# Attention gates of a hybrid layer: exp(-ln(1 + exp(-z))) per group of columns instead of one sigmoid per key head

## What is computed

```python
aq, ak, av, rq, rf_fwd, rf_bwd, ri, rg, za, zr = jnp.split(h @ w_in, IN_SPLITS, axis=-1)
...
attn = block_attention(q, k_all, v_all)
...
merged = jax.nn.sigmoid(za) * attn + jax.nn.sigmoid(zr) * rec
return merged @ w_o, k, v, S_f, S_b
```

## Time and profile before

| | |
|---|---|
| time, median of 3 runs | 2664.16 us (2663.98 to 2665.03) |
| the profiled execution, its own time | 2663.92 us |
| its span, first to last instruction | 2662.1 us |
| PE busy | 2557.1 us, 96% |
| DVE busy | 1697.6 us, 64% |
| ACT busy | 1031.3 us, 39% |
| POOL busy | 837.3 us, 31% |
| granted clock of PE over the span | 0.988 |

### The profile page before, as it was taken

How to read it: one execution, slowest core, us unless ns; L and a number is a source line. 1 busy time by engine, 2 the same in 40 slices (tenths; PEclk the granted TensorE clock), 3 DMA queues, 4 the chain that set the end, 5 groups by cost and what they waited for, 6 DMA issues and landing times. The chain is left out here.

```text
span 2662.1 us, 40132 instructions
## 1 busy us (share of the span) xinstructions
PE 2557.1 (96%) x14417; PEld 2358.6 (89%) x14417; DVE 1697.6 (64%) x2807; ACT 1031.3 (39%) x1924; POOL 837.3 (31%) x779
## 2 busy tenths in 40 slices
PE   5999999999998999999999999999999999999997
PEld 2799999999997977788778776798999999999997
DVE  4147456646748368787687677446776677766775
ACT  4233323323323257666666667423112222222214
POOL 1123132223223433433433325633322322322322
PEclk8999999999999999999999999999999999999999
DMA  8611111111111200010010012302111111111111
GB/s 319 201 33 44 36 50 42 44 33 50 36 38 31 57 19 9 25 39 9 25 47 9 1 53 62 113 31 64 40 47 39 39 47 39 39 47 39 39 32 72
DMA packets 164538, 135.94 MB, mean 51 GB/s; under 512 B 18492, under 2 KB 142300, under 8 KB 164444
## 3 DMA queue, kind: packets, MB, share of 16 engines
q1 hardware_dynamic: 163228, 129.99, 15.7%
q10 hardware_dynamic: 1216, 4.72, 0.5%
HBM read 120.41 MB, written 14.29 MB: 51 GB/s over the span
## 5 line engine op out<-in xcount | busy, mean ns | idle before, releaser
L388 PE MATMUL mix_ps<-act_hi,w_hi 128*128 128x384 f32 (+1 forms) x1320 | 444.1, 336 | 6.1 <-ACT conv L2492 3.0
L389 PE MATMUL mix_ps<-act_lo,w_hi 128*128 128x384 f32 (+1 forms) x1320 | 442.9, 336 | 0.0
L390 PE MATMUL mix_ps<-act_hi,w_lo 128*128 128x384 f32 (+1 forms) x1320 | 442.7, 335 | 0.0
L388 PE MATMUL proj_ps<-act_hi,w_hi 128*128 128x384 f32 x1152 | 406.4, 353 | 1.1 <-ACTq L741 1.1
L390 PE MATMUL proj_ps<-act_hi,w_lo 128*128 128x384 f32 x1152 | 386.5, 336 | 0.0
L389 PE MATMUL proj_ps<-act_lo,w_hi 128*128 128x384 f32 x1152 | 386.4, 335 | 0.0
L2602 DVE SCALAR_TENSOR_TENSOR resid_t<-mix_ps,mod,resid_t 128x384 f32<-128x384 f32 (+2 forms) x640 | 273.9, 508 | 134.5 <-PE mix_ps L390 134.5
L1944 DVE TENSOR_TENSOR probs_lo<-mix_ps,probs_hi 128x512 fp32r<-128x512 f32 x324 | 222.7, 688 | 142.4 <-ACT mix_ps L1739 138.8
L1738 ACT ACTIVATE probs_hi<-mix_ps 128x512 fp32r<-128x512 f32 x324 | 193.6, 598 | 183.9 <-PE mix_ps L1538 182.1
L388 PEld LDWEIGHTS mix_ps<-act_hi,w_hi 128*128 128x128 f32 x1320 | 248.8, 189 | 11.7 <-issue 5.4
L564 POOL CAST w_hi<-w_raw 128x1024 fp32r<-128x1024 f32 x48 | 79.2, 1649 | 571.2 <-PE proj_ps L390 531.3
(11 more groups left out here) (301 smaller groups left out, 5409.0 us busy)
## 6 DMA issues: line engine op xcount, KB each, us to landing
w_raw<-in_w_in SPq DMA_DIRECT2D x64, 512.0 KB, 3.8
w_raw<-in_w_up SPq DMA_DIRECT2D x44, 512.0 KB, 3.8
ada_w<-in_ada_w SPq DMA_DIRECT2D x7, 2048.0 KB, 15.8
w_raw<-in_w_down SPq DMA_DIRECT2D x22, 512.0 KB, 3.6
q_k_dec<-in_ada_w SPq DMA_DIRECT2D x5, 2048.0 KB, 8.1
out<-xy SPq DMA_DIRECT2D x9, 512.0 KB, 2.7
w_raw<-in_w_o SPq DMA_DIRECT2D x8, 512.0 KB, 5.3
xy<-in_x_sample SPq DMA_DIRECT2D x8, 512.0 KB, 6.9
```

The source lines that it names most:

```text
L388: nc.tensor.matmul(out, w_hi, x_hi, start=(k == 0), stop=False)
L389: nc.tensor.matmul(out, w_hi, x_lo, start=False, stop=False)
L390: return nc.tensor.matmul(out, w_lo, x_hi, start=False, stop=last)
```

## The change

`gate_out` and `first_gate_out` no longer copy a group out of PSUM. They write exp(-z) there, then ln(1 + x) in place, then exp(-x) in place, which together are 1 / (1 + exp(-z)). A group is so three ACT instructions of 128 by 384 instead of one, each waiting for the one before. `gate_sigmoid` and the table loads around it are gone, four sigmoids of 128 by 2304 and eight loads in all; exp and ln stay in one table. The semaphore `za_sig` now counts groups.

```diff
+                def gate_rest(kv, n, z):
+                    nc.scalar.activation(z, z, ACT.Ln, bias=1.0).then_inc(za_ln, 1)
+                    act.wait_ge(za_ln, 6 * kv + n + 1)
+                    nc.scalar.activation(z, z, ACT.Exp, scale=-1.0).then_inc(za_sig, 1)
+
                 def first_gate_out(n):
                     act.wait_ge(proj_done, NT + n + 1)
                     u, g = divmod(n, NG)
-                    nc.scalar.activation(ZA[:, u, g * G:(g + 1) * G], ps[:, B_PROJ + (NT + n) % 2, 0:G], ACT.Copy).then_inc(proj_out, 1)
+                    z = ZA[:, u, g * G:(g + 1) * G]
+                    nc.scalar.activation(z, ps[:, B_PROJ + (NT + n) % 2, 0:G], ACT.Exp, scale=-1.0).then_inc(proj_out, 1)
+                    act.wait_ge(proj_out, NT + n + 1)
+                    gate_rest(0, n, z)
 
                 def gate_out(kv, n):
                     act.wait_ge(f_done, F_AT["g", kv, n] + 1)
                     act.wait_ge(mix_ok, 2 * kv)
                     u, g = divmod(n, NG)
-                    nc.scalar.activation(ZA[:, u, g * G:(g + 1) * G], ps[:, B_F, 0:G], ACT.Copy).then_inc(f_out, 1)
+                    z = ZA[:, u, g * G:(g + 1) * G]
+                    nc.scalar.activation(z, ps[:, B_F, 0:G], ACT.Exp, scale=-1.0).then_inc(f_out, 1)
+                    act.wait_ge(f_out, F_AT["g", kv, n] + 1)
+                    gate_rest(kv, n, z)
...
-                def gate_sigmoid(kv):
-                    act.wait_ge(f_out if kv else proj_out, F_AT["g", kv, 5] + 1 if kv else NT + 6)
-                    nc.scalar.activation(ZA[:, :, :], ZA[:, :, :], ACT.Sigmoid).then_inc(za_sig, 1)
...
                     if kv:
                         inverse_ln(s - 1)
                         inverse_exp(s - 1)
-                        gate_sigmoid(kv - 1)
-                        nc.scalar.preload_act_table_set(LN_EXP)
...
-                    if s == NSTEP - 5:
-                        gate_sigmoid(NKV - 1)
-                        nc.scalar.preload_act_table_set(LN_EXP)
```

More of the change, by code:

```diff
@@ L1048, in phase2 @@
         r_ln, r_est, r_chk, r_ref, att_ok = sem("a_r_ln"), sem("a_r_est"), sem("a_r_chk"), sem("a_r_ref"), sem("a_att_ok")
-        za_sig, za_mul, rec_in, mix_ok, mix_store = sem("a_za_sig"), sem("a_za_mul"), sem("a_rec_in"), sem("a_mix_ok"), sem("a_mix_store")
+        za_ln, za_sig, za_mul, rec_in, mix_ok, mix_store = sem("a_za_ln"), sem("a_za_sig"), sem("a_za_mul"), sem("a_rec_in"), sem("a_mix_ok"), sem("a_mix_store")
         mixed_in, mh_ok, ml_ok, last_rec = sem("a_mixed_in"), sem("a_mixed_hi"), sem("a_mixed_lo"), sem("a_last_rec")
@@ L1350, in last_mix @@
                     if c == 0:
-                        pool.wait_ge(za_sig, NKV)
+                        pool.wait_ge(za_sig, 6 * NKV)
                         pool.wait_ge(last_rec, 32)
@@ L1963, in gate @@
                     dve.wait_ge(att_ok, NS * (kv + 1))
-                    dve.wait_ge(za_sig, kv + 1)
+                    dve.wait_ge(za_sig, 6 * (kv + 1))
                     for j in range(2):
@@ L2074, in last_mix @@
                     if c == 2:
-                        dve.wait_ge(za_sig, NKV)
+                        dve.wait_ge(za_sig, 6 * NKV)
                         dve.wait_ge(last_rec, 32)
```

## The result

| | median, us | runs | lowest to highest |
|---|---|---|---|
| before | 2662.57 | 20 | 2658.92 to 2667.44 |
| after | 2667.15 | 20 | 2663.49 to 2669.63 |

The ratio is 1.0013, with a 95% interval of 1.0007 to 1.0019: the change costs 3.5 us (1.9 to 5.1; the two medians of the table differ by 4.6). It is slower, as forecast, but by less than half of the forecast 9.2 us, and inside the 0.2% that was taken as "no change". The runs of one kernel spread by 4 us to either side, so the places have to be read from the traces.

A forecast was written before the change was run, and what follows sets the result against it. PE, busy 96% of the span, was taken as the bound, ACT costing only where PE waits. The terms 9.5 + 2.3 + 1.9 - 4.5 = +9.2 us gave 2673.4 us against the median of 2664.16, range 2667 to 2680.

The forecast's parts named there:

- Key head 0, the i = 4 groups and the context steps are free: Six groups of key head 0, three i = 4 groups of key head 3, three context-step sigmoids: no PE time lost or gained.
- Each group makes what is behind it later by 1.17 us: At each of 24 gate groups: ACT is held 1.63 us instead of 0.46, so what follows is 1.17 us later.
- the 0.95 us a step: Ten groups at n = 2 to 6, key heads 1 and 2: PE waits 0.85 us for `q_out`, plus 0.1 slower restart.
- In between, the steps are full on PE, so nothing recovers it: Between the ten groups of key heads 1 and 2: PE regains none of the loss, so the ten cost 9.5 us.
- The two at n = 7: Groups at n = 7, key heads 1 and 2: the whole 1.17 us reaches PE through `keys_low`, 2.3 us for both.
- The two of key head 3: Two of key head 3's three groups at i = 9 meet the same `q_out`: 0.95 us each, 1.9 us.
- The last place: Step s = 31, last sigmoid: 5.4 us of wait and slow clock go, its gate group takes 0.95; gain 4.5 us.
- Partly hidden: Rival, all groups: each adds nearer 0.9 us, the lower bound of +4.4 us, 2668.6 us, no change; chance 12%.
- Only the loads count: Rival: added instructions hide everywhere, leaving only the 5.4 us gain at the last sigmoid, 2658.8 us, faster; chance 6%.
- the last place doesn't shorten: Rival at the last sigmoid: the 4.01 us wait is DVE's backlog, gain small, losses 14.7 us, 2678.8 us; chance 6%.
- The clock did not fall behind any of the new waits: Rival claimed the opposite: PE's clock falls behind all twelve new waits, 2.6 us each, +40 us, 2704 us; chance 5%.
- The sum of all low ends: Whole kernel: lower bound +4.4 us with the clock taking off 2.5 us at once, 2666.1 us; stated range began at 2667.

## Why the prediction was right or wrong

**Right.** The places and their causes. PE waits in the ten steps at L1524 with ACT's `q_t_hilo` as releaser, at n = 7 at L1509 for `keys_low`, and at s = 31 the slow stretch is gone and the wait of 4.01 us has shrunk to 0.95, the ordinary wait of the steps behind it. Key head 0, the i = 4 groups and the context steps are free. No load remained. The durations of Ln and Exp, 0.525 us, and the distance between dependent ones (0.53 to 0.55 us from start to start) are as forecast.

**The step that failed: "Each group makes what is behind it later by 1.17 us", and with it the 0.95 us a step.** It is 0.92 us at `q_out` and 0.68 us at PE. The mechanism was right, and this term of the sum was too large. Two things were read wrongly.

- *What follows the last Exp overlaps with it.* The distance behind an instruction from SBUF to SBUF was taken from the earlier trace rows, 0.66 us behind L1749, 0.03 after its end. Here L1751 starts at 1182.30, 0.44 us behind the start of L1697 and 0.09 before its end. So the exponentials behind the group are late by 1182.30 - 1180.78 - 0.46 = 1.06 us, not 1.17. The row chosen was of 64 partitions and the new instruction has 128. That row repeats (1185.64 to 1186.30 in the kernel with the pair behind `q_out`, where PE had long delivered); why it does not overlap wasn't tested. The Trainium skill, "ScalarE: Activation LUTs", section "What ACT_TABLE_LOAD costs", gives about 93 ns of overlap for ACTIVATEs back to back; by the trace it holds for this one and not behind L1749.
- *`q_out` was not waiting for ACT alone.* Before, it started 0.63 us behind the last exponential, where these follow each other in 0.5. It was held by PE's own transposes, as PE's timeline of before shows:

```profile
1181.19 0.60 PE L1492 MATMUL mix_ps<-ident,q_stage 128*128 128x128 f32 x4
```

They end at 1181.79 and `q_out` starts at 1181.82. So 0.13 us of the delay meet a wait that was there in any case; after, the distance is 1183.29 - 1182.77 = 0.52 us.

Together they make 1.17 - 0.92 = 0.25 of the 0.27 us between the 0.95 and the 0.68; the slack and the restart were as read. Only the wait that the profile would show was read wrongly besides: with 1.17 us of delay it would have been 0.85 - 0.16 = 0.69 us, not 0.85, for the reason given beside the 0.43.

**A second step that failed: "In between, the steps are full on PE, so nothing recovers it".** That was read from one stretch, with n = 2 in it. The steps at n = 4 have a wait of 0.56 us for a row maximum, which takes up all of a group's loss: two of the ten cost nothing. Ten at 0.95 were 9.5 us; they are 8 at 0.68 and 2 at 0, 5.5 us. This term holds 4.0 of the 5.1 us between the sum of the forecast, +9.2, and the +4.1 of the table: 2.6 for the size of a step's loss in all ten, and 1.4 for the two steps that lose nothing.

**The other terms.** The two at n = 7: 2.07 against 2.3. The two of key head 3: 1.44 against 1.9. The last place: -4.90 against -4.5, since it pays 0.9 for its own group (the difference between 5.80, where the pair stands elsewhere, and 4.90) and would give back 5.8 instead of the 5.4 that were read from the neighbouring step; its length is 18.39 us, 18.8 had been said.

**The rivals.** "Partly hidden" had nearly the right amount: 0.93 us added, 0.61 a step, +4.4 us in sum. That the sum comes so close to +4.1 is in part luck: it has thirteen places at 0.61, where eight lose 0.68, two 0.72 and the last 0.9, and two lose nothing. It was given 12%, because the end of the bounds was held for unlikely although the trace of before shows that overlap behind most of ACT's instructions. "Only the loads count" and "the last place doesn't shorten" are excluded by the step table. The clock did not fall behind any of the new waits, of 0.43 and 1.26 us, in either trace.

**The range.** It began at 2667.0, and the median is 2667.15, inside by 0.15 us, which is luck where runs spread by 4 us to either side. The sum of all low ends was 2666.1 and was cut off there. Of the 6.3 us between 2673.4 and the median, 1.6 are not the change's at all: the median of before was 2664.16 in the three runs given and is 2662.57 in twenty.

## What to carry to other kernels

Take the time between two instructions of an in-order engine from a row of the same kind (partitions, memories, dependent or not), and ask of the row before whether the later one was waiting for another engine: if so, that wait is slack which the queue's delay meets first. Read the waits of every step in which the cost would recur, not of one and a multiplier. If an edit puts work ahead of an instruction that PE is about to need, move the work into a gap of the same engine behind it before judging the edit: the same instructions cost 3.5 us in one place and gained 6.9 in another.

## What the runs showed of the hardware that was not expected

- The loss on PE is linear in ACT's delay behind a slack of 0.24 us (0.36, 0.86, 0.92 and 1.47 us late: 0.12, 0.61, 0.68 and 1.24 lost), and zero in steps with a wait of 0.56 us of their own until that is used up.
- Behind a wait of 1.81 us the clock fell from the 2.4 GHz level to that of 1.2 GHz for part of a step, at the same place where it did not behind one of 1.26; that made 3.1 us out of 1.6. It fell around a wait of 2.2 us in step s = 28 in all fourteen traces, and in none behind the 1.42 us at L1509 in key head 0. In the context step of key head 3, with waits of 1.2 and 0.6 us, it fell in some traces and not in others of the same kernel, and likewise in the first context step, with waits of 0.99, 0.19 and 0.42 us. What decides there is open.
- A table load costs its 1.283 us and the overlaps at its ends: the two around the last sigmoid 2.84 us together, about 1.4 each.
- Steps of untouched code repeat within 0.1 us between traces where the clock does, while whole runs spread by 8 us. For a change this small the step table decides what the totals can't.
